# Where two input buffers and an activation buffer begin in SBUF: 128 and 96 bytes behind a multiple of 512 in place of 64

## The chip, the core and the metric

The kernel runs on one core of a Trainium2 chip. The metric is the device time of one execution in microseconds (us), the median of several runs. TensorE (PE) multiplies, ScalarE (ACT), VectorE (DVE) and GpSimd (POOL) do the rest, and SyncE (SP) issues the DMAs. SBUF, the on-chip memory, has 128 partitions; every tensor of the program has an address inside a partition, the same in all of them.

## What is computed

Three blocks of a transformer-like network, one after the other, on 256 tokens of width 1024 in float32:

```
for i in range(DEPTH):                       # first_block, DEPTH = 2
    h = rmsnorm(x, norm_mixer[i])
    if i % N_MIXERS == 0:
        mix = short_conv_mixer(h, ...)
    else:
        mix = swa_sink_attention(h, ...)     # 16 heads of 64, 4 kv heads
    x = x + mix
    h = rmsnorm(x, norm_ffn[i])
    x = x + swiglu_ffn(h, ...)               # silu(g) * u, width 2816
...
u = rms_norm(h, attn_pre_norm[l])            # second_block, one layer
mix = hybrid_mixer(u, ...)                   # attention of 8 heads of 128, and an RG-LRU
h = h + rms_norm(mix, attn_post_norm[l])
u = rms_norm(h, mlp_pre_norm[l])
m = jnp.square(jax.nn.relu(u @ w_mlp_up[l])) @ w_mlp_down[l]
h = h + rms_norm(m, mlp_post_norm[l])
```

Nearly all arithmetic is in the products with the weight matrices, 180 MB of weights that are read once.

## The kernel before

**Tensors.** The tokens lie along the free dimension, the width along the partitions: a normed input is eight k-tiles of 128 partitions x 256 tokens. A float32 product is made of three products of a cheaper type, fp32r: every operand is split into a rounded part hi and a remainder lo, and hi x hi, hi x lo and lo x hi are summed in PSUM. So the input buffers `xa` and `xb` are [128, 8, 2, 256]: for each k-tile 256 elements hi and 256 elements lo, 2048 bytes. `ghid` (line 166) has the same form with 22 k-tiles and holds the inner activations of the two gated MLPs, `hid` (line 154) with 32 k-tiles those of the last MLP. Weights arrive by DMA in `raw` (line 119); for each piece of 8 k-tiles x 128 columns ACT writes the rounded part to `whi` and DVE the remainder to `wlo` (lines 120 and 121), four slots of 4096 bytes each.

**Addresses.** The build gives tensors addresses in the order of their allocation (lines 118 to 200). 1152 bytes are taken before the first one. `before_raw` (384 bytes) puts `raw` at 1536, a multiple of 512; `whi` at 34304, `wlo` at 50688 and `x` at 67072 are multiples of 512 too. `before_xa` (line 123, 16 floats) puts `xa` at 75328 and `xb` at 91712, both 64 bytes behind a multiple of 512. `spill`, `z`, `act1`, `gate`, `sq`, `ssum`, `lnms`, `rbc`, `vecs`, `cons` and smaller ones follow. `before_region` (line 152, 56 floats) fills up to 140288, a multiple of 512, from where several layouts share the same bytes at different times: `hid`; `before_ghid` (16 floats) and `ghid` at 140352, 64 behind a multiple of 512; `u` and `cv`; the tensors of the first attention, in which `unused1` (line 183) moves `bias` behind the end of `ghid`; and those of the hybrid mixer, from `q2` on.

**Matmuls.** `blocks` (line 509) makes a narrow product with 256 columns: for a pair of k-tiles whi x hi (line 520), whi x lo (522), then wlo x hi (524). Where the accumulator is wide (`dst.shape[1] == 2 * TOK`) whi x hi and whi x lo are one matmul of 512 columns (line 518), and whole tiles of eight k-tiles go through `whole_tile` (line 489): 6 wide matmuls on line 497, 8 narrow ones on line 495, and two each on lines 504 and 505. In all of these the weights are the stationary operand and the input moves. `unit` (line 554) turns this round, for the value projection of the second attention ("v2") and the down projection of the last MLP ("mdn"): the input is stationary and 512 columns of weights move (lines 560 to 562). One has `xa`, the other `hid`.

**Order.** The stages follow the table `BODIES` (line 44): bx, c and o are the convolution mixer, up0 and dn0 its gated MLP, qkv and wo the first attention, up1 and dn1 its MLP, x2 to out2 the hybrid mixer, mup and mdn the last MLP. Each stage has bodies of four pieces; PE waits for a piece's `lo_ready` and for a free bank of a ring of four (`emptied`). The narrow form is used in the long gate/up stages after the first `WIDE_BODIES` bodies, in both gated downs (`gated_down`, line 619, on `ghid`), in c, o, wo, ba and bl, and in the gates of the LRU. The heads of the second attention stand between whole tiles of g2, ga and gl (`beside`, line 910).

Of the kernel before, what the change touches and what calls it, by code (L numbers as in the profile page):

```python
# [20 lines left out]
F32 = mybir.dt.float32  # L21
# [5 lines left out]
P = 128  # L27
TOK = 256
# [84 lines left out]
def build(nc, bias_in_dram, x_in, stream, vecs_in, sinks_in, cons_in, out):  # L113
    with ExitStack() as ctx:
        sb = lambda n, s, d=F32: ctx.enter_context(nc.sbuf_tensor(n, s, d))
# [4 lines left out]
        whi = sb("whi", [P, 4, 8, P], F32R)  # L120
        wlo = sb("wlo", [P, 4, 8, P], F32R)
        x = sb("x", [P, KT, TOK])
        sb("before_xa", [P, 16])
        xa = sb("xa", [P, KT, 2, TOK], F32R)
        xb = sb("xb", [P, KT, 2, TOK], F32R)
        spill = sb("spill", [P, 4, TOK])
# [22 lines left out]
        den = sb("den", [P, 2, 4])  # L149
        rden = sb("rden", [P, 2, 4])  # L150

        sb("before_region", [P, 56])
        region = ExitStack()
        hid = region.enter_context(nc.sbuf_tensor("hid", [P, 32, 2, TOK], F32R))
        mt = region.enter_context(nc.sbuf_tensor("mt", [P, 2, D], F32))
# [6 lines left out]
        region.close()  # L162

        regiond = ExitStack()
        regiond.enter_context(nc.sbuf_tensor("before_ghid", [P, 16], F32))
        ghid = regiond.enter_context(nc.sbuf_tensor("ghid", [P, FT, 2, TOK], F32R))
        regiond.close()
        region0 = ExitStack()
# [4 lines left out]
        sb1 = lambda n, s: region1.enter_context(nc.sbuf_tensor(n, s, F32))  # L173
# [6 lines left out]
        pt1 = sb1("pt1", [P, 2, 3 * P])  # L180
        lnq = sb1("lnq", [P, 32])
        rq = sb1("rq", [P, 32])
        sb1("unused1", [P, 22 * 2 * TOK - (12 + 2 + 2 + 2) * TOK - 2 * 2 * 2 * 386 - 2 * 384 - 64 + 16])
        bias = sb1("bias", [P, HEADS1, 3 * P])
        region1.close()
        region2 = ExitStack()
# [2234 lines left out]
```

How the kernel before makes its waits and increments, by code:

```python
        @block.sync  # L406
# [10 lines left out]
            def load(b, h, offset, size, waits):  # L417
                if waits:
                    if h == 1:
                        sp.wait_ge(lo_ready, 4 * b - 4)
                    sp.wait_ge(raw_loaded[h], 16 * b)
                    if h == 0:
                        sp.wait_ge(lo_ready, 4 * b - 6)
                    sp.wait_ge(x_loaded[3], 16)
                src = stream[bass.ds(offset, P * size)].rearrange("(p n) -> p n", p=P)
                sp.dma_start(raw[:, (b % 2) * 2 + h, 0:size], src).then_inc(raw_loaded[h], 16)
# [1 line left out]
            def load_half(b, h, chunks):  # L428
                if h == 1:
                    sp.wait_ge(lo_ready, 4 * b - 4)
                sp.wait_ge(raw_loaded[h], 16 * b)
                if in_units.index(b) > 0:
                    sp.wait_ge(unit_loaded[h], 16 * in_units.index(b))
                if h == 0:
                    sp.wait_ge(lo_ready, 4 * b - 6)
                dst = raw[:, (b % 2) * 2 + h, :].rearrange("p (g m k) -> p g m k", g=2, m=2)
                for g, loaded in enumerate((raw_loaded, unit_loaded)):
                    sp.dma_start(dst[:, g, :, :], chunks[:, g, :, h * 4 * P:(h + 1) * 4 * P]).then_inc(loaded[h], 16)
# [6 lines left out]
            for h in range(2):
                sp.wait_ge(raw_loaded[h], 16)
                if h == 0:
# [31 lines left out]
                sp.wait_ge(done, count)  # L482
                sp.dma_start(out[:, tiles, t * P:(t + 1) * P], x[:, tiles, t * P:(t + 1) * P]).then_inc(stored, 16)
            sp.wait_ge(stored, 16 * 5)
```

## Time and profile before

| | us |
|---|---|
| median of 3 runs | 978.49 (978.38 to 978.63) |
| the profiled execution, whole | 978.66 |
| its span, first to last instruction | 976.9 |
| PE busy | 970.0, 7208 matmuls |
| PE weight loads busy | 908.3 |
| DVE busy | 696.7 |
| ACT busy | 589.4 |
| POOL busy | 268.8 |
| share of PE in the chain that ended last | 97% |
| DMA | 180.94 MB, 185 GB/s mean |

The busy time of an engine is the union of its instructions. Matmuls overlap: a record begins where the matmul begins and ends, by a model, where its last result is written, so its duration is longer than the distance to the next start. A count of starts in a stretch, or the distance between two starts in the timeline, tells the pace. The timeline merges neighbours on the same line into one row, with its count behind the x.

### The profile page before, as it was taken

The numbers are of one execution on the slowest core, as the hardware profiler recorded it, in microseconds if no ns is written. First come the engines' busy times: TensorE is split into PE (matmuls) and PEld (weight loads), VectorE is DVE, ScalarE is ACT, GpSimd is POOL, SyncE is SP. The second block draws the span as 40 slices with busy tenths as digits, with TensorE's granted clock in tenths as the row PEclk, the third lists the DMA queues.
The fourth block names the chain that finished last, engine by engine and source line by source line (L and its number), as shares of the span: only waits on it lengthen the run. The fifth ranks groups of instructions, "written<-read, shape, count | busy, mean of one in ns | idle before, by whom it ended". The sixth has DMA issues, their size and how long they took to land.

```text
span 976.9 us, 20204 instructions
## 1 busy us (share of the span) xinstructions
PE 970.0 (99%) x7208; PEld 908.3 (93%) x7208; DVE 696.7 (71%) x1046; ACT 589.4 (60%) x1050; POOL 268.8 (28%) x241
## 2 busy tenths in 40 slices
PE   9999999999999999999999999999999999999998
PEld 7999999999998899999999899889989989998887
DVE  7987866665668778666565799987867877664443
ACT  7556755554557767545554578968585577664332
POOL 2431233220102223223210146542031546441000
PEclk9999999999999999999999999999999999999999
DMA  9785555655543245555455554654444536556531
GB/s 334 257 312 189 190 210 177 209 170 192 205 172 130 88 135 211 198 189 200 166 204 205 174 177 167 216 178 166 171 146 169 205 130 218 205 179 207 182 130 43
DMA packets 37713, 180.94 MB, mean 185 GB/s; under 512 B 3472, under 2 KB 7824, under 8 KB 19984
## 3 DMA queue, kind: packets, MB, share of 16 engines
q1 hardware_dynamic: 37504, 179.99, 52.8%
q8 instruction: 41, 0.67, 0.3%
q14 instruction: 24, 0.20, 0.1%
q10 hardware_dynamic: 144, 0.08, 0.0%
HBM read 179.01 MB, written 1.05 MB: 184 GB/s over the span
## 4 chain that ended last, share of the span: by engine, by line
PE 97%; ACT 1%; DVE 1%; POOL 1%; DMA 1%; issue 0%; SPq 0%; POOLq 0%; DVEq 0%
PE bank L524 20%; PE bank L520 17%; PE bank L522 17%; PE bank L497 9%; PE bank L518 7%; PE bank L495 6%; PE bank L561 4%; PE bank L562 4%; PE bank L560 4%; PE bank L505 2%; PE bank L504 2%; PE bank L773 1%; PE bank L648 1%; DMA x<-in_x 1%; PE bank L757 1%; PE bank L787 0%
## 5 line engine op out<-in xcount | busy, mean ns | idle before, releaser
L1556 DVE TENSOR_TENSOR wlo<-raw,whi 128x1024 fp32r<-128x1024 f32 (+1 forms) x289 | 354.1, 1225 | 147.9 <-ACT whi L1031 146.9
L1031 ACT ACTIVATE whi<-raw 128x1024 fp32r<-128x1024 f32 (+2 forms) x289 | 302.1, 1046 | 202.0 <-PE bank L524 195.4
L524 PE MATMUL bank<-xa,wlo 128*128 128x256 f32 x1200 | 242.3, 277 | 0.0
L520 PE MATMUL bank<-xa,whi 128*128 128x256 f32 x904 | 227.3, 276 | 0.0
L522 PE MATMUL bank<-xa,whi 128*128 128x256 f32 x904 | 227.1, 276 | 0.0
L524 PEld LDWEIGHTS bank<-xa,wlo 128*128 128x128 f32 x1200 | 191.6, 188 | 9.0
L520 PEld LDWEIGHTS bank<-xa,whi 128*128 128x128 f32 x904 | 169.7, 188 | 0.0
L522 PEld LDWEIGHTS bank<-xa,whi 128*128 128x128 f32 x904 | 169.7, 188 | 0.0
L2152 POOL TENSOR_TENSOR gate<-act,rbc 128x256 f32<-128x256 f32 x44 | 68.9, 1567 | 158.2 <-ACT act L1196 153.0
L518 PE MATMUL bank<-xa,whi 128*128 128x512 f32 x296 | 98.9, 402 | 0.6 <-POOL wlo L2264 0.5
L520 PE MATMUL bank<-ghid,whi 128*128 128x256 f32 x352 | 88.5, 276 | 0.0
L522 PE MATMUL bank<-ghid,whi 128*128 128x256 f32 x352 | 88.4, 276 | 0.0
L1564 DVE TENSOR_TENSOR wlo<-raw,whi 128x1024 fp32r<-128x1024 f32 x40 | 49.2, 1231 | 45.9 <-ACT whi L1040 45.9
L1040 ACT ACTIVATE whi<-raw 128x1024 fp32r<-128x1024 f32 x40 | 42.4, 1066 | 49.3 <-PE bank L562 40.0
L497 PE MATMUL bank<-xa,whi 128*128 128x512 f32 x252 | 71.9, 394 | 0.0
L524 PE MATMUL bank<-ghid,wlo 128*128 128x256 f32 x352 | 68.5, 276 | 0.0
L520 PEld LDWEIGHTS bank<-ghid,whi 128*128 128x128 f32 x352 | 66.1, 188 | 0.0
L522 PEld LDWEIGHTS bank<-ghid,whi 128*128 128x128 f32 x352 | 66.1, 188 | 0.0
L495 PE MATMUL bank<-xa,wlo 128*128 128x256 f32 x336 | 65.6, 276 | 0.0
L2133 POOL TENSOR_TENSOR ssum<-ssum,sq 128x256 f32<-128x256 f32 x39 | 35.9, 921 | 106.2 <-ACT sq L1072 105.6
L1062 ACT ACTIVATE spill<-bank 128x256 f32<-128x256 f32 x95 | 36.1, 380 | 46.2 <-PE bank L495 39.2
L495 PEld LDWEIGHTS bank<-xa,wlo 128*128 128x128 f32 x336 | 56.9, 188 | 7.2
(247 smaller groups left out, 1873.4 us busy)
## 6 DMA issues: line engine op xcount, KB each, us to landing
raw<-in_stream SPq DMA_DIRECT2D x137, 1024.0 KB, 4.8
raw<-in_stream SPq DMA_DIRECT2D x42, 512.0 KB, 5.0
raw<-in_stream SPq DMA_DIRECT2D x8, 768.0 KB, 4.2
bias<-in_bias SPq DMA_DIRECT2D x1, 3072.0 KB, 11.5
raw<-in_stream SPq DMA_DIRECT2D x8, 256.0 KB, 5.7
x<-in_x SPq DMA_DIRECT2D x4, 256.0 KB, 5.6
out<-x SPq DMA_DIRECT2D x3, 256.0 KB, 2.2
cons<-in_cons SPq DMA_DIRECT2D x1, 576.0 KB, 8.9
```

The lines of the kernel that those rows point to most:

```text
L495: return pe.matmul(narrow, wlo[:, slot, k, :], X[:, k, 0, :], start=False, stop=k == KT - 1)
L497: pe.matmul(dst, whi[:, slot, k, :], X[:, k, :, :], start=k == 0, stop=False)
L518: pe.matmul(dst, whi[:, slot, at + i, :], X[:, k, :, :], start=first and i == 0, stop=False)
L520: pe.matmul(narrow, whi[:, slot, at + i, :], X[:, k, 0, :], start=first and i == 0, stop=False)
L522: pe.matmul(narrow, whi[:, slot, at + i, :], X[:, k, 1, :], start=False, stop=False)
L524: ins = pe.matmul(narrow, wlo[:, slot, at + i, :], X[:, k, 0, :], start=False, stop=last and i == len(tiles) - 1)
L560: pe.matmul(dst[:, :], X[:, k0 + k, 0, cols], hi, start=first and k == 0, stop=False)
L1031: act.activation(whi[:, p, 0:kts, :].rearrange("p k m -> p (k m)"), src, ACT.Copy)\
L1040: act.activation(whi[:, p, :, :].rearrange("p (k m) c -> p k m c", k=2), k_pairs(raw[:, (b % 2) * 2 + p // 2, :], p % 2), ACT.Copy).then_i ...
L1556: dve.tensor_tensor(wlo[:, p, 0:kts, :].rearrange("p k m -> p (k m)"), src, whi[:, p, 0:kts, :].rearrange("p k m -> p (k m)").bitcast(F32) ...
L1564: dve.tensor_tensor(wlo[:, p, :, :].rearrange("p (k m) c -> p k m c", k=2), k_pairs(raw[:, (b % 2) * 2 + p // 2, :], p % 2), whi[:, p, :, ...
L2152: pool.tensor_tensor(gate[:, m, :], act1[:, m, :], rbc[:], ALU.mult).then_inc(gate_ready, 1)
```

## The change

Four fillers change their size. `before_xa` grows from 16 to 32 floats, so that `xa` and `xb` begin 128 bytes behind a multiple of 512, and all tensors between `xb` and the region lie 64 bytes higher. `before_region` shrinks from 56 to 40 floats, so that the region begins where it did. `before_ghid` grows from 16 to 24 floats: `ghid` begins 96 bytes behind a multiple of 512. `unused1` grows by 8 floats, so that `bias` still lies behind the end of `ghid`, 32 bytes higher. No instruction is added, removed or moved.

```diff
-        sb("before_xa", [P, 16])
+        sb("before_xa", [P, 32])
         xa = sb("xa", [P, KT, 2, TOK], F32R)
         xb = sb("xb", [P, KT, 2, TOK], F32R)
...
-        sb("before_region", [P, 56])
+        sb("before_region", [P, 40])
...
-        regiond.enter_context(nc.sbuf_tensor("before_ghid", [P, 16], F32))
+        regiond.enter_context(nc.sbuf_tensor("before_ghid", [P, 24], F32))
         ghid = regiond.enter_context(nc.sbuf_tensor("ghid", [P, FT, 2, TOK], F32R))
...
-        sb1("unused1", [P, 22 * 2 * TOK - (12 + 2 + 2 + 2) * TOK - 2 * 2 * 2 * 386 - 2 * 384 - 64 + 16])
+        sb1("unused1", [P, 22 * 2 * TOK - (12 + 2 + 2 + 2) * TOK - 2 * 2 * 2 * 386 - 2 * 384 - 64 + 24])
```

## Rows read from the trace of the kernel before

**Rows 1.** The page: busy time of the engines, and the last chain by engine
```profile
PE 970.0 (99%) x7208; PEld 908.3 (93%) x7208; DVE 696.7 (71%) x1046; ACT 589.4 (60%) x1050; POOL 268.8 (28%) x241
...
PE 97%; ACT 1%; DVE 1%; POOL 1%; DMA 1%; issue 0%; SPq 0%; POOLq 0%; DVEq 0%
```

**Rows 2.** Windows: busy us and instructions (x) of each engine, clock, DMA
```profile
core 0: us, PE busy (x) PEld busy (x) DVE busy (x) ACT busy (x) POOL busy (x), PEclk, DMA share, GB/s
150.00:200.00 50.00, 50.00 (x444) 50.00 (x443) 33.43 (x48) 24.67 (x37) 14.61 (x9) 1.00 0.57 198
200.00:250.00 50.00, 50.00 (x443) 50.00 (x443) 32.15 (x50) 26.63 (x38) 8.15 (x7) 1.00 0.54 184
```

**Rows 3.** Groups by form: busy us, mean ns of one, idle before
```profile
L524 PE MATMUL bank<-xa,wlo 128*128 128x256 f32 x1200 | 242.3, 277 | 0.0
L520 PE MATMUL bank<-xa,whi 128*128 128x256 f32 x904 | 227.3, 276 | 0.0
...
L518 PE MATMUL bank<-xa,whi 128*128 128x512 f32 x296 | 98.9, 402 | 0.6 <-POOL wlo L2264 0.5
...
L497 PE MATMUL bank<-xa,whi 128*128 128x512 f32 x252 | 71.9, 394 | 0.0
...
L524 PE MATMUL bank<-ghid,wlo 128*128 128x256 f32 x352 | 68.5, 276 | 0.0
...
L495 PE MATMUL bank<-xa,wlo 128*128 128x256 f32 x336 | 65.6, 276 | 0.0
...
L560 PE MATMUL bank<-whi,hid 128*128 128x512 f32 x128 | 49.9, 390 | 0.0
...
L524 PE MATMUL bank<-xb,wlo 128*128 128x256 f32 x224 | 47.3, 277 | 0.0
L497 PE MATMUL bank<-xb,whi 128*128 128x512 f32 x144 | 43.7, 411 | 0.0
```

**Rows 4.** Timeline of PE, 256 columns on xb: start us, us, line, count
```profile
79.75 0.28 PE L520 MATMUL bank<-xb,whi 128*128 128x256 f32 x1
...
81.45 0.28 PE L520 MATMUL bank<-xb,whi 128*128 128x256 f32 x1
```

**Rows 5.** Timeline of PE, the same lines at about 350 us
```profile
350.62 0.28 PE L520 MATMUL bank<-xb,whi 128*128 128x256 f32 x1
...
351.80 0.28 PE L520 MATMUL bank<-xb,whi 128*128 128x256 f32 x1
```

**Rows 6.** Windows over two stretches of 256-column matmuls on xb
```profile
350.50:358.50 8.00, 8.00 (x69) 8.00 (x69) 8.00 (x12) 5.41 (x11) 2.69 (x4) 1.00 0.67 226
604.00:618.00 14.00, 13.90 (x110) 13.35 (x110) 13.66 (x19) 13.07 (x25) 9.87 (x10) 1.00 0.59 194
```

**Rows 7.** Timeline of PE, `unit` with hid as the stationary operand
```profile
930.15 0.39 PE L562 MATMUL bank<-whi,hid 128*128 128x512 f32 x1
...
932.87 0.39 PE L562 MATMUL bank<-whi,hid 128*128 128x512 f32 x1
```

**Rows 8.** Timeline of PE, `unit` with xa as the stationary operand
```profile
621.10 0.40 PE L562 MATMUL bank<-whi,xa 128*128 128x512 f32 x1
...
623.90 0.40 PE L562 MATMUL bank<-whi,xa 128*128 128x512 f32 x1
```

**Rows 9.** Timeline of PE, one whole tile on xa
```profile
581.75 0.85 PE L497 MATMUL bank<-xa,whi 128*128 128x512 f32 x3
...
584.49 0.39 PE L497 MATMUL bank<-xa,whi 128*128 128x512 f32 x1
```

**Rows 10.** Timeline of PE, one whole tile on xb and what follows
```profile
641.59 0.85 PE L497 MATMUL bank<-xb,whi 128*128 128x512 f32 x3
...
644.39 0.39 PE L879 MATMUL bank<-k,q 128*128 128x128 f32 x2
```

**Rows 11.** Timeline of PE, pairs on line 518, xa
```profile
725.01 0.62 PE L518 MATMUL bank<-xa,whi 128*128 128x512 f32 x2
...
727.77 0.39 PE L518 MATMUL bank<-xa,whi 128*128 128x512 f32 x1
```

## Prediction

> **What bounds the kernel now.** Read the page's shares first, then its chain of work that ended last. TensorE (PE) is busy 970.0 of 976.9 us with 7208 matmuls, and 97% of the chain is PE [rows 1]. The windows view says the same of two long stretches: PE is occupied for all 50.00 us, the granted clock is 1.00 (the 2.4 GHz level), and 444 and 443 matmuls start in each, while DVE works 33 us and ACT 25 us of the 50 [rows 2]. So nothing is waited for there; the end is set by how many matmuls there are and how far apart they start. The view by form tells the duration of one matmul, 276 ns for the 256-column forms and 389 to 411 ns for the 512-column ones [rows 3], but a duration contains the latency in which the next one already runs. The spacing of the starts is what counts, and it is read from the timeline.
>
> There are two spacings. In a clean run on xb fifteen 256-column matmuls start between 79.75 and 81.45 us: 1.70 us, 113.3 ns each [rows 4]. On the same lines, with the same buffer, weights and clock, ten start between 350.62 and 351.80 us: 118 ns each [rows 5], and this lasts through a stretch of 8.00 us with 69 matmuls in it [rows 6], against 71 at the clean spacing. Both spacings go on by themselves: PE holds one until something shifts it.
>
> **What the change touches.** It adds, removes and moves no instruction, DMA or semaphore. It shifts addresses inside each partition. xa and xb go from 64 to 128 bytes behind a multiple of 512, ghid from 64 to 96, and the small tensors between xb and the region (spill, z, act1, gate, the norm's tensors, cons, rcos, upsq and others) go up by 64 bytes with them. raw, whi, wlo and x stay at a multiple of 512, and so does hid, since before_region shrinks by the same 16 floats. bias moves by 32 bytes.
>
> Step 1, the engines beside PE: 0 us. Each DVE, ACT and POOL instruction could get some ns longer or shorter, but PE is occupied throughout while DVE is at 67% and ACT at 50% of the stretch [rows 2]. That slack hides it. The cover is missing in the gaps between stages: the page has 976.9 - 970.0 = 6.9 us without PE [rows 1], a few of them at the start and the end, and a change of some per cent in the engines there is 0.1 to 0.3 us either way. No queue gets longer and no wait is added.
>
> Step 2, the price of the relation of the addresses. A matmul reads two operands: the moving one streams by while the stationary one of the next matmul is loaded. In all blocks the stationary operand is whi or wlo (0 behind a multiple of 512) and the moving one xa, xb or ghid (+64). In `unit` the roles are turned: whi and wlo move, and xa (v2) or hid (mdn) is stationary. That gives an experiment which the trace already holds. With hid, both operands at 0, twelve matmuls of 512 columns start in 932.87 - 930.15 = 2.72 us, 226.7 ns each [rows 7]. With xa, stationary at +64, the same three lines take 623.90 - 621.10 = 2.80 us, 233.3 ns each, and never recover [rows 8]. 226.7 is twice 113.3, so I call 113.3 ns per 256 columns the clean pace and count whatever is above it. Two things differ between rows 7 and 8, the offset and what went before, so rows 7 and 8 suggest that the offset matters and don't prove it.
>
> Step 3, what the present offset costs over the clean pace, stage by stage.
> - Whole tiles on xa (`whole_tile`, 6 wide and 12 narrow matmuls, 24 units of 113.3 ns = 2.72 us): one takes 584.49 - 581.75 = 2.74 us [rows 9]. L497 has 252 of them on xa [rows 3], 42 tiles x 0.02 = 0.8 us.
> - Whole tiles on xb beside the heads of the second attention: 644.39 - 641.59 = 2.80 us [rows 10]; 144 / 6 = 24 tiles x 0.08 = 1.9 us.
> - Pairs on line 518: from 725.01 to 727.77 us there are 8 wide and 8 narrow, 24 units, in 2.76 us [rows 11]; 296 / 8 = 37 such groups x 0.04 = 1.5 us.
> - Narrow stretches at 118 ns: 14 us of the LRU gates with 110 matmuls [rows 6] and about as many around 350 us, some 220 x 4.7 ns = 1.0 us.
> - v2: 96 x 6.6 ns = 0.6 us.
> The sum is 5.8 us. This is what a better offset can give back, at most 0.6% of the time. The large blocks, gate/up narrow, both downs on ghid and the down on hid, already run at the clean pace [rows 2, 4, 7].
>
> Step 4, what the offset can cost. No row shows +128, +96 or -128. From below the bound is the 5.8 us of step 3 regained. From above it is that the narrow matmuls which are clean now run at the 118 ns of rows 5. Their count from the groups by form: on xa 1200 + 2 x 904 + 336, on ghid 3 x 352, on xb 3 x 224 (lines 520 and 522 count alike throughout) and some 450 in smaller groups, 5500 in all [rows 3]. Some 700 of them are slow already by the stretches above (220, and about ten in each xb tile and in the pairs of line 518), so 4800 x 4.7 ns = +22.6 us. For ghid alone it is 1056 x 4.7 = +5.0 us.
>
> Which value? The nearest rows are 7 and 8: relation 0 falls back to the clean pace and keeps it, relation -64 stays slow, and +64 holds either pace. If the operands collide by a repeating pattern of the addresses, +128 may lie where 0 lies (a pattern of 128 bytes) or further into the bad side (a pattern of 512, in which the moving operand, read twice as fast, meets the other one earlier). The rows don't decide it. I take half of the regainable sum, since after each group of f32 transposes and sums (attention, norms) PE is thrown out of step anyway and needs a few matmuls to settle: -3 us. Then ghid: its 1056 matmuls are all clean now, so at +96 it can only stay or lose; I take 0.
>
> Sum against the profiled execution, span 976.9 us and 978.66 us in all (1.8 us around it): -3 gives 973.9 us of span, 975.7 in all. The median of the runs, 978.49, lies 0.2 below the profiled one, hence 975.5.
>
> What the skill says against this: the Trainium skill, "TensorE: Matmul & The Clock Gate", section "Part 2: What happens when you issue a matmul", says that loading the next weights takes nothing from the running matmul's reads, since PE has two independent read ports. By it the offsets are worth nothing and the time stays 978.5. Rows 4 and 5, the same instruction at the same clock 4% apart, show that something between the matmuls does cost time, though not that it is the ports.
>
> **The rivals.**
> *Nothing happens.* The two paces come from how the sequencer or the array falls into step after a disturbance, and no address has a part in it. For it: rows 4 and 5 have the same offsets and both paces. Against it: rows 7 and 8. It gives 978.5, within 1.5 us, as each disturbance may fall out differently.
> *ghid alone loses.* Its offset is only a multiple of 32, which no moving operand of this type has now. Place: dn0 and dn1. Price: 1056 x 4.7 = +5.0 us, from which at most 2 us of gain elsewhere come off: 981.5 to 983.5. It decides from the point at which the 24 pieces of a down stage start their matmuls over 115 ns apart.
> *The clean pace is lost on xa too.* The moving operand meets the stationary one earlier in each matmul, in every narrow block. Price +22.6 us: 1001. It decides from about 1060 narrow matmuls that leave the clean pace: 5.0 us, the forecast's gain and the 2 us that can be measured.
> *The pace of 113.3 itself falls.* 256 columns at 2.4 GHz are 106.7 ns, so 6.7 ns of each unit are something else. If the offset had a part in that, 5500 narrow matmuls alone would give tens of us. The pace is the same at 0 and at +64 [rows 4, 7], which speaks against it.
>
> **How the numbers follow.** Faster by part of the 5.8 us: 0.43, mostly 972.5 to 976.5. Nothing: 0.25. ghid alone or a small loss elsewhere, 980.5 to 984: 0.14. xa too: 0.15. The pace falls: 0.03. The range 971.8 to 984.5 holds the first three, 0.82, and leaves out the last two. A measurement of this kernel can tell about 0.2%, 2 us, from no change. Faster: 0.43 + 0.03, less 0.02 for gains under 2 us: 0.44. Same: 0.25 + 0.02, less 0.01: 0.26. Slower: 0.30.
>
> **What would show it.** In the profile after, the starts in the gate/up and down stretches should stay 113.3 ns apart (444 matmuls in 50 us); fewer than 430 there is the third rival, in the down stretch alone the second. The forecast is right for its reason if v2's twelve matmuls come down from 2.80 towards 2.72 us, the xb whole tiles from 2.80 and the pairs of line 518 from 2.76. If these three are unchanged and the time too, addresses play no part. The prediction is wrong if the pace changes in a stretch whose offsets did not change (mdn on hid), or if the time moves in the gaps without PE.

## The result, and the profile after

The changed kernel takes 1007.55 us (1006.89 to 1007.88), the kernel before 978.56 beside it: a ratio of 1.0294, 95% interval 1.0282 to 1.0306. It is 29 us slower. The forecast was 975.5 in a range of 971.8 to 984.5; the time came out near the rival that the prediction put at 1001, "the clean pace is lost on xa too", to which it gave 0.15.

The page of the changed kernel, its shares and its chain by engine, which answer to [rows 1]:

```profile
PE 998.7 (99%) x7208; PEld 936.7 (93%) x7208; DVE 697.0 (69%) x1046; ACT 589.7 (59%) x1050; POOL 265.1 (26%) x241
...
PE 98%; DVE 1%; ACT 1%; issue 0%; POOL 0%; POOLq 0%
```

The span grew from 976.9 to 1004.9 us, 28.0 us, and PE's busy time from 970.0 to 998.7 with the same 7208 matmuls. The 6.2 us without PE are not where the time went.

The windows of the changed kernel, of the first gate/up stage, of the first down stage on ghid, of the second gate/up stage and of the LRU's gates (busy us and instructions of PE, PEld, DVE, ACT and POOL, clock, DMA), which answer to [rows 2, 6]:

```profile
core 0: us, PE busy (x) PEld busy (x) DVE busy (x) ACT busy (x) POOL busy (x), PEclk, DMA share, GB/s
150.00:200.00 50.00, 50.00 (x423) 50.00 (x423) 30.96 (x44) 24.58 (x36) 15.40 (x10) 1.00 0.51 180
230.00:270.00 40.00, 40.00 (x336) 40.00 (x335) 22.74 (x33) 18.42 (x26) 2.67 (x3) 1.00 0.49 172
420.00:470.00 50.00, 50.00 (x419) 50.00 (x419) 30.81 (x44) 24.30 (x36) 15.03 (x9) 1.00 0.54 189
620.00:634.00 14.00, 14.00 (x102) 13.21 (x102) 13.79 (x21) 11.95 (x23) 10.67 (x10) 1.00 0.56 185
```

And of the kernel before, two stretches not shown so far, a narrow one on xb (stage o) and the down stage on ghid:

```profile
77.00:92.00 15.00, 15.00 (x135) 15.00 (x134) 10.64 (x15) 9.18 (x16) 2.69 (x4) 1.00 0.46 155
230.00:270.00 40.00, 40.00 (x356) 40.00 (x355) 24.95 (x33) 20.07 (x29) 4.59 (x5) 1.00 0.59 201
```

A window counts each matmul that touches it, so the distance of two starts is the window's length plus one duration of 0.28 us, divided by the count: 50.28 / 444 = 113.2 ns on xa before and 50.28 / 423 = 118.9 ns after; on ghid 40.28 / 356 = 113.1 before and 40.28 / 336 = 119.9 after. One matmul more or less in a window is 0.3 ns, so smaller differences between such paces mean nothing. The second gate/up stage, with the same buffers at the same addresses as the first, has 50.28 / 419 = 120.0 ns: the new distance has more than one pace on xa. Clock 1.00 in all of them. DVE and ACT do no more than before (30.96 and 24.58 us of 50 against 33.43 and 24.67), they get less work because PE asks for less.

The groups by form of the changed kernel (mean ns of one), which answer to [rows 3]:

```profile
L524 PE MATMUL bank<-xa,wlo 128*128 128x256 f32 x1200 | 247.9, 282 | 0.0
L522 PE MATMUL bank<-xa,whi 128*128 128x256 f32 x904 | 235.2, 282 | 0.0
...
L520 PE MATMUL bank<-ghid,whi 128*128 128x256 f32 x352 | 92.4, 285 | 0.0
L522 PE MATMUL bank<-ghid,whi 128*128 128x256 f32 x352 | 91.3, 279 | 0.0
...
L524 PE MATMUL bank<-ghid,wlo 128*128 128x256 f32 x352 | 70.7, 282 | 0.0
...
L560 PE MATMUL bank<-whi,hid 128*128 128x512 f32 x128 | 49.9, 390 | 0.0
```

The narrow products on xa went from 276 to 282 ns. On ghid the three lines no longer agree, 285, 279 and 282. hid, whose address did not change, keeps 390. Three rows of the timeline of PE in the gate/up stage (start us, us, line, count), six starts apart, answer to [rows 4]:

```profile
179.85 0.28 PE L520 MATMUL bank<-xa,whi 128*128 128x256 f32 x1
...
180.56 0.28 PE L520 MATMUL bank<-xa,whi 128*128 128x256 f32 x1
...
181.28 0.28 PE L520 MATMUL bank<-xa,whi 128*128 128x256 f32 x1
```

From 179.85 to 181.28 us twelve matmuls start: 1.43 us, 119 ns each, and the clean 113.3 ns is found nowhere in this stage.

One whole tile on xa after [rows 9] is 601.00 - 598.16 = 2.84 us against 2.74:

```profile
598.16 0.87 PE L497 MATMUL bank<-xa,whi 128*128 128x512 f32 x3
...
601.00 0.86 PE L497 MATMUL bank<-xa,whi 128*128 128x512 f32 x3
```

v2, `unit` with xa stationary, now at 128 [rows 8]: 647.05 - 644.27 = 2.78 us for twelve, 231.7 ns each, against 233.3:

```profile
644.27 0.39 PE L560 MATMUL bank<-whi,xa 128*128 128x512 f32 x1
...
647.05 0.40 PE L560 MATMUL bank<-whi,xa 128*128 128x512 f32 x1
```

mdn, `unit` with hid, whose offsets are as before [rows 7]: 957.34 - 954.62 = 2.72 us, unchanged:

```profile
954.62 0.39 PE L561 MATMUL bank<-wlo,hid 128*128 128x512 f32 x1
...
957.34 0.39 PE L561 MATMUL bank<-wlo,hid 128*128 128x512 f32 x1
```

Where the 28 us came from, with the distances from each matmul's start to the next one's added up over both traces: the 3544 narrow matmuls on xa take 18.1 us more, the 1056 on ghid 7.0, the 960 narrow ones on xb 2.5, the wide ones on xa and xb together 0.4; v2 gives back 0.1. That is the whole 28 us.

### The profile page after: what moved, and what is told of

Its sections match the earlier page's. It is cut to its first block, busy times and chain, and to the rows that moved or that the text cites. A ratio compares the mean times of both kernels' runs of the same rounds, so it can differ in the third digit from the quotient of the medians.

```text
span 1004.9 us, 20204 instructions
## 1 busy us (share of the span) xinstructions
PE 998.7 (99%) x7208; PEld 936.7 (93%) x7208; DVE 697.0 (69%) x1046; ACT 589.7 (59%) x1050; POOL 265.1 (26%) x241
## 4 chain that ended last, share of the span: by engine, by line
PE 98%; DVE 1%; ACT 1%; issue 0%; POOL 0%; POOLq 0%
PE bank L524 21%; PE bank L520 18%; PE bank L522 17%; PE bank L497 9%; PE bank L518 7%; PE bank L495 6%; PE bank L561 4%; PE bank L560 4%; PE bank L562 4%; PE bank L505 2%; PE bank L504 2%; PE bank L648 1%; PE bank L773 1%; PE bank L757 1%; PE bank L787 0%; PE bank L637 0%
## 5 line engine op out<-in xcount | busy, mean ns | idle before, releaser
L524 PE MATMUL bank<-xa,wlo 128*128 128x256 f32 x1200 | 247.9, 282 | 0.0
L522 PE MATMUL bank<-xa,whi 128*128 128x256 f32 x904 | 235.2, 282 | 0.0
L520 PE MATMUL bank<-xa,whi 128*128 128x256 f32 x904 | 235.1, 282 | 0.0
L524 PEld LDWEIGHTS bank<-xa,wlo 128*128 128x128 f32 x1200 | 194.8, 188 | 9.0
L520 PE MATMUL bank<-ghid,whi 128*128 128x256 f32 x352 | 92.4, 285 | 0.0
L522 PE MATMUL bank<-ghid,whi 128*128 128x256 f32 x352 | 91.3, 279 | 0.0
L524 PE MATMUL bank<-ghid,wlo 128*128 128x256 f32 x352 | 70.7, 282 | 0.0
L495 PE MATMUL bank<-xa,wlo 128*128 128x256 f32 x336 | 67.4, 282 | 0.0
L495 PEld LDWEIGHTS bank<-xa,wlo 128*128 128x128 f32 x336 | 57.6, 189 | 7.5
```

The costliest lines, as they stand in the source:

```text
L495: return pe.matmul(narrow, wlo[:, slot, k, :], X[:, k, 0, :], start=False, stop=k == KT - 1)
L520: pe.matmul(narrow, whi[:, slot, at + i, :], X[:, k, 0, :], start=first and i == 0, stop=False)
L522: pe.matmul(narrow, whi[:, slot, at + i, :], X[:, k, 1, :], start=False, stop=False)
L524: ins = pe.matmul(narrow, wlo[:, slot, at + i, :], X[:, k, 0, :], start=False, stop=last and i == len(tiles) - 1)
```

## The experiments

Each kernel is the one before with other fillers; offsets are given in bytes behind a multiple of 512. "Distance" is the moving operand's offset less the stationary one's. Paces are of the windows from 150 to 200 us (gate/up, xa) and 230 to 270 us (down, ghid), by the division above; where a kernel's rows are not shown they come from the same two windows of it.

### Which of the moved tensors counts

**The inputs alone.** xa and xb at 128, ghid at 64, the tensors behind xb at their old offset:

```diff
-        sb("before_xa", [P, 16])
+        sb("before_xa", [P, 32])
...
+        sb("before_spill", [P, 112])
         spill = sb("spill", [P, 4, TOK])
```

> xa and xb begin 128 bytes behind a multiple of 512; the small tensors behind them keep their 64 (a filler of 448 bytes behind xb), ghid keeps 64. Theory A, the operands of the matmuls: 1007.55 less what ghid brought, about 7 us, so 1000 to 1001; the down stages of the gated MLPs start 256-column matmuls 113.3 ns apart again (222 in 25 us), all other narrow stages about 119 ns. Theory B, the small tensors (spill, z, cons and so on) that moved by 64 bytes: 978.5 plus the 7 us of ghid at most. Theory C, no address matters: 1007 is not explained, time as before, 978.5.

Measured 1005.22 us, ratio 1.0272 (1.0242 to 1.0302). The two windows:

```profile
150.00:200.00 50.00, 50.00 (x419) 50.00 (x418) 30.86 (x44) 23.95 (x35) 15.70 (x10) 1.00 0.50 180
230.00:270.00 40.00, 40.00 (x342) 40.00 (x342) 22.70 (x34) 18.43 (x26) 2.68 (x3) 1.00 0.52 182
```

xa's pace is 50.28 / 419 = 120.0 ns, where the changed kernel has 118.9 in the same window at the same distance. And ghid, at its old distance of 64, has 40.28 / 342 = 117.8 ns and not 113.3, though ghid and the weights stand at the very addresses that they had in the kernel before. The expectation missed by 4 to 5 us, and 1056 x 4.5 ns is 4.8 us. This is taken up below.

**ghid alone.**

```diff
-        regiond.enter_context(nc.sbuf_tensor("before_ghid", [P, 16], F32))
+        regiond.enter_context(nc.sbuf_tensor("before_ghid", [P, 24], F32))
```

> Only ghid is moved, from 64 to 96 bytes behind a multiple of 512. Theory A: the 1056 matmuls on ghid go from 113.3 to 120 ns, 978.5 + 7.0 = 985.5, nothing else changes. Theory B and C: 978.5.

Measured 985.42 us, ratio 1.0071 (1.0048 to 1.0094), as theory A said:

```profile
150.00:200.00 50.00, 50.00 (x444) 50.00 (x443) 33.10 (x48) 25.21 (x37) 15.05 (x9) 1.00 0.57 201
230.00:270.00 40.00, 40.00 (x336) 40.00 (x335) 24.22 (x33) 19.58 (x28) 4.55 (x5) 1.00 0.56 198
```

xa keeps 444 matmuls in 50 us; ghid goes to 40.28 / 336 = 119.9 ns.

**The small tensors alone.**

```diff
+        sb("before_spill", [P, 16])
         spill = sb("spill", [P, 4, TOK])
...
-        sb("before_region", [P, 56])
+        sb("before_region", [P, 40])
```

> xa, xb and ghid stay at 64; all tensors between xb and the region go up by 64 bytes, as in the change. Theory A: 978.5, within 1 us. Theory B: most of the 29 us, so 1000 or more, or with ghid's 7 us taken off about 1000.

Measured 978.81 us, ratio 1.0002 (0.9991 to 1.0014). Step 1 of the prediction, the engines beside PE, holds: what DVE, ACT and POOL read and write may move by 64 bytes at no cost.

```profile
150.00:200.00 50.00, 50.00 (x444) 50.00 (x443) 33.41 (x48) 24.58 (x36) 14.46 (x9) 1.00 0.57 199
230.00:270.00 40.00, 40.00 (x355) 40.00 (x354) 24.94 (x33) 20.06 (x29) 4.57 (x5) 1.00 0.57 200
```

### Its own offset, or the distance to the weights

xa, xb and ghid at 128, and whi and wlo at 64, so that the distance is 64 again:

```diff
+        sb("before_whi", [P, 16])
         whi = sb("whi", [P, 4, 8, P], F32R)
         wlo = sb("wlo", [P, 4, 8, P], F32R)
+        sb("before_x", [P, 112])
         x = sb("x", [P, KT, TOK])
-        sb("before_xa", [P, 16])
+        sb("before_xa", [P, 32])
...
-        regiond.enter_context(nc.sbuf_tensor("before_ghid", [P, 16], F32))
+        regiond.enter_context(nc.sbuf_tensor("before_ghid", [P, 32], F32))
```

> xa, xb and ghid at 128, and whi and wlo at 64 in place of 0, so that the moving operand is again 64 bytes ahead of the stationary one in every narrow matmul. If the distance between the two operands counts (they collide): all narrow stages are back at 113.3 ns and the time is that of before but for the down projection of the last MLP, where the weights at 64 now move over hid at 0: 978 to 982. If the moving operand's own offset counts: as after, 1000 to 1008.

Measured 979.57 us, ratio 1.0011 (0.9999 to 1.0022). Both narrow stages are back:

```profile
150.00:200.00 50.00, 50.00 (x444) 50.00 (x443) 33.16 (x48) 25.15 (x37) 15.05 (x9) 1.00 0.57 201
230.00:270.00 40.00, 40.00 (x356) 40.00 (x355) 24.82 (x34) 19.89 (x28) 4.57 (x5) 1.00 0.59 200
```

With inputs at 128 the time is 1005 us when the weights are at 0 and 979.6 when they are at 64 (ghid was moved along with the weights, so that its distance is 64 in both kernels). xa has the same offset in both, and its pace goes from 120.0 to 113.2 ns. So the offset of the moving operand by itself is not what counts, the distance between the two operands is. The one stage whose distance got worse shows it from the other side: in mdn the weights at 64 now move over hid at 0, and twelve matmuls take 932.76 - 930.01 = 2.75 us instead of 2.72:

```profile
930.01 0.39 PE L563 MATMUL bank<-whi,hid 128*128 128x512 f32 x1
...
932.76 0.39 PE L563 MATMUL bank<-whi,hid 128*128 128x512 f32 x1
```

Over 384 matmuls that is 384 x 2.3 ns = 0.9 us, the whole difference to the kernel before.

### The map of distances

The same fillers with other sizes, xa, xb and ghid together; for 48, 56, 72 and 80 the tensors begin at 32 and a view begins some floats into them:

```diff
-        xa = sb("xa", [P, KT, 2, TOK], F32R)
+        LEAD = 4          # 6, 10 and 12 for 56, 72 and 80
+        xa = sb("xa", [P, 2 * KT * TOK + 128], F32R)[:, LEAD:LEAD + 2 * KT * TOK]\
+            .rearrange("p (k h t) -> p k h t", k=KT, h=2)
```

> xa, xb and ghid begin at a multiple of 512, so moving and stationary operand are at distance 0 everywhere; the small tensors stay at 64. Theory P128 (the pattern that collides repeats every 128 bytes): 0 is like 128, so about 119 ns on xa and 1005 us. Theory P512 (the distance within 512 bytes counts, and the moving operand may be a little ahead): 0 is on the good side or at its edge; mdn, with both operands at 0, ran clean in the kernel before, so 972 to 979, v2 at 226.7 ns, if the edge is not overstepped, and above 990 if it is.

> xa, xb and ghid at 32. Both theories put 32 between 0 and 64: 973 to 979, better than before if the slow pace is left sooner after each disturbance; the 0.6 us of v2 shrink too. If whole multiples of 64 were what counts, as 96 for ghid might also say, about 1010.

> xa, xb and ghid at 192. P128: 192 is like 64, so 978.5. P512: the operands still meet inside each load, as at 128, so 1000 to 1015.

> xa, xb and ghid at 320. A pattern of 256 bytes: like 64, 978.5. P128: 978.5 too. P512: they meet in the middle of each load, 1000 to 1015.

> xa and xb at 96, ghid at 160. The distance counts modulo 256 (0: 1008.5, 32: 995.3, 64: 978.6, 128: 1005 to 1008, 192: 999.3, 320: 978.6). If 64 is a narrow good place between bad ones, xa's narrow matmuls take about 120 ns at 96, as ghid's did, and the time is 1000 to 1010; if 96 was bad for ghid alone because it is no multiple of 64, xa shows the same, and 32 should have been as bad as 96, which it was not. For ghid at 160 between 128 and 192: 118 to 120 ns.

> xa at 160, xb and ghid at 224. The points that are missing between 128 and 256. Between 192 (117.7 ns) and 256 = 0 (120 ns) nothing clean is expected: 118 to 120 ns on ghid and xa, 998 to 1008 us. A second clean distance on this side, the mirror of 64, would show as 113.3 ns on ghid and xb.

> xa, xb and ghid 48 bytes behind a multiple of 512, by views that begin 16 bytes into a tensor at 32. Between 32 (3.3 to 3.8 ns over the clean pace) and 64 (0 to 0.45): if the price rises evenly, 985 to 988; if the clean place is a window, 48 is either clean (976 to 979, and better than before if the slow pace is left sooner) or like 32.

> The same at 80. Between 64 and 96 (6.7 ns on ghid): evenly 990 to 995; as a window 976 to 979 or 1005.

> xa, xb and ghid at 56 (48 gave 1001.8, 64 gives 978.5). If the clean pace needs 64 itself, about 1000; if its window reaches below 64, 976 to 979, and if a disturbed PE comes back sooner there, the best version so far: 978.5 less part of the 6 us of excess.

> The same at 72 (80 gave 1009.9). If the clean pace needs 64 itself, 1005 to 1010; if the window reaches above 64, 973 to 979.

| distance | us | ratio (95%) | ns on xa | ns on ghid |
|---|---|---|---|---|
| 0 | 1008.54 | 1.0304 (1.0274 to 1.0334) | 120.0 | 120.2 |
| 32 | 995.26 | 1.0169 (1.0139 to 1.0198) | 116.7 | 116.4 |
| 48 | 1001.83 | 1.0234 (1.0190 to 1.0278) | 118.3 | 118.5 |
| 56 | 1011.49 | 1.0338 (1.0308 to 1.0368) | 120.0 | 120.2 |
| 64, the kernel before | 978.5 | 1 | 113.2 | 113.1 |
| 72 | 1016.85 | 1.0392 (1.0362 to 1.0423) | 121.2 | 121.0 |
| 80 | 1009.88 | 1.0317 (1.0272 to 1.0361) | 120.0 | 120.2 |
| 96 (ghid 160) | 1009.65 | 1.0314 (1.0270 to 1.0359) | 120.0 | 118.8 |
| 128 (ghid 96), the change (a) | 1007.55 | 1.0294 (1.0282 to 1.0306) | 118.9 | 119.9 |
| 160 (xb and ghid 224) | 1000.37 | 1.0219 (1.0175 to 1.0263) | 117.5 | 118.5 |
| 192 | 999.25 | 1.0209 (1.0180 to 1.0239) | 117.8 | 117.8 |
| 320 | 978.61 | 1.0000 (0.9989 to 1.0011) | 113.5 | 113.1 |

(a) xa's pace is that of the first gate/up stage; the second one has 120.0. Each pace in the table is that of one stage, and 128 with ghid at 64 is the kernel of the inputs alone: 1005.22 us, 120.0 and 117.8 ns.

The expectations of 0, 96, 160, 192 and 320 named two or more outcomes each, and the time fell near one of them. Four missed upwards: 32 (973 to 979 us or about 1010, measured 995.3), 48 (985 to 988, 976 to 979, or like 32, measured 1001.8), 56 (about 1000 at the worst, measured 1011.5) and 72 (1005 to 1010 at the worst, measured 1016.9); 80 came out 5 us above its worst case.

Three kernels' windows, at 0, 320 and 72:

```profile
150.00:200.00 50.00, 50.00 (x419) 50.00 (x418) 31.27 (x44) 23.21 (x34) 16.16 (x10) 1.00 0.52 185
230.00:270.00 40.00, 40.00 (x335) 40.00 (x335) 22.05 (x34) 17.99 (x25) 2.69 (x3) 1.00 0.54 188
```

```profile
150.00:200.00 50.00, 50.00 (x443) 50.00 (x443) 33.28 (x48) 25.04 (x37) 14.98 (x9) 1.00 0.57 201
230.00:270.00 40.00, 40.00 (x356) 40.00 (x355) 24.84 (x34) 19.99 (x28) 4.57 (x5) 1.00 0.58 201
```

```profile
150.00:200.00 50.00, 50.00 (x415) 50.00 (x415) 30.67 (x43) 23.85 (x35) 14.97 (x9) 1.00 0.53 187
230.00:270.00 40.00, 40.00 (x333) 40.00 (x332) 22.57 (x37) 18.75 (x26) 2.66 (x3) 1.00 0.49 168
```

Two things follow. First, 320 is as good as 64, while 0, 128 and 192 are not. Of the repeats that the expectations named only 256 bytes fits the times, since one of 128 would make 192 good, and one of 512 would not make 320 good. (A repeat of 256 rests on this one pair, 64 and 320.) Second, around 64 the good place is a point, not a window: at 56 and 72, eight bytes to either side, narrow matmuls take 120 and 121 ns.

The value for 192 needs a reservation. In that kernel xb is at 192 like xa, and stages o, up0 and dn0 run at 117.8 ns, but in the narrow stretch around 360 us PE holds the clean pace at this very distance:

```profile
361.18 0.28 PE L521 MATMUL bank<-xb,whi 128*128 128x256 f32 x1
...
366.62 0.28 PE L521 MATMUL bank<-xb,whi 128*128 128x256 f32 x1
```

Between these two starts lie 48 matmuls, 5.44 / 48 = 113.3 ns each; it goes on from 359.9 to 368.0 us, some 70 matmuls. So 192 has the same two paces as 64, and the 20 us between the two kernels come from which of them the long stages run at. Whether the long stages would keep the clean pace at 192, were they entered in it, no run tries; a repeat of 128 in the paces that are possible is therefore not excluded. At 0, 32, 48, 56, 72, 80, 96, 128, 160 and 224 no twelve narrow matmuls in a row run clean anywhere in these traces.

Distances that are no multiple of 16 bytes, 56 and 72, are worse than their neighbours 48 and 80 (1011.5 and 1016.9 us against 1001.8 and 1009.9). The Trainium skill, "SBUF — State Buffer", section "Specifications (TRN2)", gives SBUF lines of 16 bytes with a penalty for each step to a new one; these two pairs agree with it in direction, and no run shows that it is the cause. Neither an even rise nor a rule of whole 32 or 64 bytes describes the table. None of the other distances beats the kernel before.

At distance 0 v2 does become clean: 652.66 - 649.94 = 2.72 us for twelve matmuls, 226.7 ns, as mdn has always had at distance 0 [rows 7], and [rows 8] had 2.80:

```profile
649.94 0.39 PE L560 MATMUL bank<-wlo,xa 128*128 128x512 f32 x1
...
652.66 0.39 PE L560 MATMUL bank<-wlo,xa 128*128 128x512 f32 x1
```

So `unit`, where 512 columns move per load of 128, wants distance 0, and the narrow matmuls, 256 columns per load, want 64. One rule for both forms does not exist in these runs. Nor does v2 bear out a repeat of 256: in the kernel at 192 its distance is -192, which would be the same as 64, and twelve matmuls take 2.80 us, where mdn at 64 takes 2.75.

That the other engines' reads and writes of SBUF set these paces is spoken against by their steadiness: in the kernel at 0 the narrow matmuls of the gate/up and down stages are 120 ns apart in every group of twelve, while DVE works 31 us and ACT 23 us of the 50.

### Why ghid was slow at its good distance

Two kernels ask whether a pace is carried over or follows from the layout. xb alone at 128:

```diff
+        sb("before_xb", [P, 16])
         xb = sb("xb", [P, KT, 2, TOK], F32R)
+        sb("before_spill", [P, 112])
         spill = sb("spill", [P, 4, TOK])
```

> Only xb goes to 128; xa and ghid stay at 64. If each stage's pace follows from its own distance: xb's 672 narrow and 288 + 144 tile matmuls rise by about 4 and 2 ns, +3.5 us, and xa and ghid stay as before: 982. If a slow pace is carried over into a stage whose distance is good, up0 or up1, which follow on xb's stages o and wo, are slow too: up to 1320 narrow matmuls x 4.5 = 6 us per stage more, 988 to 994.

Measured 981.32 us, ratio 1.0031 (1.0019 to 1.0042), near the 982 of the first case. Its windows in stage o (xb), gate/up (xa) and down (ghid):

```profile
77.00:92.00 15.00, 15.00 (x129) 15.00 (x127) 10.35 (x14) 8.91 (x16) 2.40 (x3) 1.00 0.44 150
150.00:200.00 50.00, 50.00 (x443) 50.00 (x443) 32.90 (x47) 25.16 (x38) 13.62 (x9) 1.00 0.56 193
230.00:270.00 40.00, 40.00 (x356) 40.00 (x355) 25.61 (x35) 20.18 (x28) 4.58 (x5) 1.00 0.58 198
```

xb has 15.28 / 129 = 118.4 ns where the kernel before has 15.28 / 135 = 113.2, and xa and ghid stay clean. Here nothing was carried over. Between o and the narrow part of up0 stand up0's first bodies with 512-column matmuls on xa at distance 64; that PE comes back to the clean pace in them fits, but is not shown apart.

The other one is the kernel of the inputs alone with f32 matmuls thrown in ahead of each column group of the gated downs, which directly follow the narrow, slow part of the up stage:

```diff
+                    if c == 0 and m == 0:
+                        for _ in range(g + 1):
+                            pe.matmul(bank[ATT][:, 0:TOK], con("ones", P), cons[:, 0:TOK], start=True, stop=True)
                     if c == 0:
                         pe.wait_ge(emptied, tile - 3)
```

> As the run with the inputs alone at 128 (1005.2 us; ghid at 64, and yet 117.8 ns), with 1, 2, 3 and 4 extra f32 matmuls of 256 columns ahead of the four column groups of each gated down; their results are not used. They cost 20 x 0.43 = 8.6 us. If ghid's slow pace there is a state carried over from the up stage, they break it in some of the eight groups, after which 113.3 ns holds: ghid's mean falls from 4.45 to between 0 and 3 ns over the clean pace. If it is a property of the addresses in that layout, it stays at 4.45.

Measured 1013.71 us, ratio 1.0357 (1.0324 to 1.0390). The timeline of PE at the start of dn1 (start us, us, line, count), where the extra matmul is on line 632 and has two records:

```profile
500.07 0.40 PE L525 MATMUL bank<-xa,wlo 128*128 128x256 f32 x2
500.30 0.60 PE L632 MATMUL bank<-cons 128*128 128x256 f32 x2
500.55 0.47 PE L521 MATMUL bank<-ghid,whi 128*128 128x256 f32 x1
500.86 0.28 PE L523 MATMUL bank<-ghid,whi 128*128 128x256 f32 x1
...
501.88 0.39 PE L525 MATMUL bank<-ghid,wlo 128*128 128x256 f32 x2
```

After one extra matmul ghid runs clean: from 500.86 to 501.88 us nine matmuls start, 113.3 ns each. The group lasts until the next disturbance, two extra matmuls at about 516 us, and then:

```profile
519.04 0.28 PE L523 MATMUL bank<-ghid,whi 128*128 128x256 f32 x1
...
520.93 0.28 PE L523 MATMUL bank<-ghid,whi 128*128 128x256 f32 x1
```

Sixteen starts from 519.04 to 520.93 us, 118 ns each. Of the eight groups of 132 matmuls this one ran at 113.3 ns and the seven others at 117.8, by the distances of their starts. The expectation that the mean would fall below 3 ns over the clean pace was missed (it fell from 4.45 to 3.9); what it was to tell apart is settled all the same, because one group is enough: in one kernel, with the same buffer at the same addresses, the same lines run at 113.3 or at 117.8 ns. One disturbance of eight brought the clean pace, and the next one ended it; the first group of dn0, behind one extra matmul as well, stayed slow, so what decides the outcome is open. At distance 64 there are two paces, each of which holds itself up.

That ghid is slow in the kernel of the inputs alone because the stage ahead of it is slow is an inference: its addresses are those of the kernel before, and in every kernel in which xa runs clean, ghid at distance 64 or 320 runs clean too. What is handed on is not the number, since xa runs at 120.0 and ghid behind it at 117.8. Other distances have more than one pace as well: at 32 xa has 116.7 ns in both gate/up stages and 117.8 in the up stage of the last MLP, at 128 it has 118.9 and 120.0, and 192 was told above. At 0, 56, 80 and 96 only one was seen on xa, 120 ns.

### Own weights, or the next ones

wlo alone at 64, so that whi is at distance 64 and wlo at 0:

```diff
+        sb("before_wlo", [P, 16])
         wlo = sb("wlo", [P, 4, 8, P], F32R)
+        sb("before_x", [P, 112])
         x = sb("x", [P, KT, TOK])
```

> The kernel before with wlo alone at 64, so that whi is at distance 64 and wlo at distance 0. If the moving operand collides with the load of the NEXT matmul's weights: in the repeating order 520 522 520 522 524 524 the matmuls that run while wlo is loaded (the second 522 and the first 524) are the long ones, and the time lies between 978.5 and the 1008.5 of distance 0 everywhere, 985 to 1000. If it collides with its own weights, lines 524 are the long ones alone. If the weights' place has no part, 978.5.

Measured 1001.46 us, ratio 1.0232 (1.0202 to 1.0262):

```profile
150.00:200.00 50.00, 50.00 (x426) 50.00 (x426) 31.63 (x44) 23.76 (x36) 15.00 (x9) 1.00 0.53 183
230.00:270.00 40.00, 40.00 (x342) 40.00 (x341) 23.60 (x35) 19.70 (x27) 3.65 (x4) 1.00 0.52 181
```

The weights' place does have a part, and one third of the products at distance 0 is enough to lose the clean pace in both stages: 118.0 ns on xa, 117.8 on ghid. It costs mdn too: there wlo moves at distance 64 over hid and whi at 0, and 384 matmuls take 89.2 us instead of 87.2, 232 ns each, more than with both weights at 64 (229). Which narrow matmuls are the long ones fits neither reading: in the first gate/up stage the distances to the next start, at the six places of the order 520 522 520 522 524 524, are 9, 4, 5, 4, 5 and 2 ns over 113. Whether the moving operand meets the load of its own weights' successor or something else stays open.

## Why the prediction was wrong

**The bound** was read rightly: PE's pace alone sets the time, no wait and no other engine has a part, and the small tensors cost nothing (978.81 with them alone moved).

**Step 2, the relation of addresses, was right in kind.** Distance counts, not the offset by itself: 1005 against 979.6 us with the weights moved along. It is not the whole, since at 64, 128 and 192 PE has more than one pace. The sentence that rows 7 and 8 "suggest that the offset matters" was borne out by v2 at distance 0, 226.7 ns.

**Step 4 is the step that failed, in its choice of a value.** "The nearest rows are 7 and 8: relation 0 falls back to the clean pace and keeps it" was read from `unit`, a different form: 512 moving columns per weight load, and with the roles turned. Carried over to the narrow form it was false: at distance 0 these take 120 ns, as slow as at 128. The case of "+128 may lie where 0 lies" came out nearly true, and it costs 30 us (1008.54) and does not save 3. The same step had both ends, -5.8 and +22.6 us, and said that the rows don't decide; it then took a value near the lower end and gave the upper one 0.15, though one sentence named the reason for it (operands that meet earlier). With one known good point and no row on the form in question, the upper end should have had most of the chance.

**The size of the upper end** was short as well: the term was 4800 x 4.7 = 22.6 us, and 28.0 were measured. The 4.7 ns was that of the second pace at distance 64 [rows 5]. At the new distances the paces are 118.9 and 120.0 ns on xa and 119.9 on ghid, 5.6 to 6.7 over the clean one, and the matmuls on xb, part of them slow before, got slower too, by 2.5 us.

**The lower end, -5.8 us,** has no support in the runs. No distance beats the kernel before. Of the parts of step 3 only v2's 0.6 us came back, at distance 0, and some 70 narrow matmuls on xb at about 350 us, 0.3 us: at 192, and at the old 64 when only the small tensors moved (72 matmuls from 350.5 to 358.5 us against 69), so that no distance is needed for it. Some readings of step 3 were off. A window of 8.00 us at the clean pace counts 8.28 / 0.1133 = 73 matmuls, not 71. The 110 matmuls in 14 us at the LRU gates are no measure of 118 ns: wide ones and idle time are among them, and the narrow ones are 125 ns apart on average. And the one xb tile of 2.80 us is a fast one: the 24 take 2.90 us on average before and 2.93 after.

**ghid: "at +96 it can only stay or lose; I take 0"** took the wrong one of the two. It lost 6.8 us by itself (985.42 against 978.59), where the rival had 5.0, with the same borrowed 4.7 ns.

**What showed it** worked as written: fewer than 430 matmuls in 50 us was named as the mark of the third rival, and there are 423. Of the three signs of the forecast's reason v2 came down a little, from 2.80 to 2.78 us, and not to 2.72; the same xb tile went from 2.80 to 2.81 and the same group of pairs on line 518 from 2.76 to 2.79. The tiles on xa went from 2.74 to 2.84.

**The rule of the skill.** The Trainium skill, "TensorE: Matmul & The Clock Gate", "Part 2: What happens when you issue a matmul", says that loading the next weights does not take bandwidth from the running matmul, because PE has two independent read ports. By it the time stays 978.5. The runs differ from it: with fp32r operands, the clock granted in full and nothing waited for, moving the weights by 64 bytes (and ghid with them, at the same distance) is worth 25 us (1005.22 against 979.57, with ghid's part of 5 us in it). The measurement decides: here the place of the two operands relative to each other costs up to 8 ns on top of each 113 ns. That it happens at the ports is not shown, and no run here tries another type.

## What to carry over

In a kernel that is bound by back-to-back matmuls of fp32r, look at the distance between starts and compare it stage by stage: two paces of the same instruction at the same clock mean that something besides the instruction count is to be had or lost. Look at every stage before a pace is put down to an address: one stage can run at the slow one of two. Treat the addresses of the moving and the stationary operand as one setting: keep their distance when any filler, tensor or buffer ahead of them changes size, and measure a distance for the form (columns per weight load) that is to use it. A value that is good for one form is no evidence for another, and when a change leaves a point that is known to be good for one that no row covers, the loss deserves the larger chance.

## What the runs showed that was not expected

- A distance of 64 bytes between fp32r operands gives 113.2 ns per matmul of 256 columns, 56 or 72 bytes 120 and 121 ns, 320 bytes 113.5 again.
- Matmuls of 512 columns with the roles turned have their good place at 0 (226.7 ns); at 64 they take 229 ns (mdn) and at -64 233.3 ns (v2). With one of the two weight buffers at 0 and the other at 64 mdn takes 232 ns, more than at either.
- At distance 64 PE can hold two paces, 113.3 and 117.8 ns, each for over a hundred matmuls. Of eight groups on ghid behind a few f32 matmuls one ran at the first and seven at the second, in one kernel. ghid at its good distance lost 4.7 us in both downs together when only the stage ahead of it was slow.
- At distance 192, where all long stages run at 117.8 ns, some 70 matmuls on xb run at 113.3 after the attention.
- The clean pace itself, 113.3 ns for 256 columns, is 6.7 ns over 256 / 2.4 GHz. No distance brought it lower.
